# Gathering the first expert pair's tokens bank by bank, and requesting the third weight buffer in three parts

## The reference

```python
h = x + jnp.concatenate([a, c], axis=-1) @ w_out       # 1024 x 1024
return h + hier_moe(rms_norm(h, g_norm_ffn), ...)

def hier_moe(xn, w_router_group, w_router_expert, w_gate, w_up, w_down):
    t = xn.reshape(-1, D_MODEL)                        # 520 tokens
    lg = (t @ w_router_group)                          # 4 groups, top 1
    le = (t @ w_router_expert)                         # 8 experts in a group, top 2
    ...
    def expert_step(acc, ew):                          # 32 experts, 1024 -> 256 -> 1024
        wg, wu, wd, cw = ew
        h = jax.nn.silu(t @ wg) * (t @ wu)
        return acc + cw[:, None] * (h @ wd), None
```

## Time and profile before

| | |
|---|---|
| median of 3 runs | 611.67 us (610.62 to 613.29) |
| the profiled execution | 607.84 us, of which the span of instructions is 606.1 |
| PE busy | 553.9 us (91%) |
| DVE, ACT, POOL busy | 278.1, 166.8, 119.2 us |
| moved by DMA | 163.48 MB, mean 270 GB/s; HBM read 151.06 MB |

### The profile page before, as it was taken

One profiled execution on the slowest core, in us unless ns is written; L12 is line 12 of the kernel. 1 busy time (PEld: TensorE's weight loads), 2 busy tenths in 40 slices (PEclk: granted clock), 3 DMA queues, 4 the chain that ended last, 5 costly groups with the idle time before them and its releaser, 6 DMA issues.

```text
span 606.1 us, 8209 instructions
## 1 busy us (share of the span) xinstructions
PE 553.9 (91%) x2944; PEld 332.5 (55%) x2944; DVE 278.1 (46%) x681; ACT 166.8 (28%) x365; POOL 119.2 (20%) x124
## 2 busy tenths in 40 slices
PE   6999999998999999899999999999996869687992
PEld 4798899887675888744555853333332313232320
DVE  5887667968314787524358731111210111111256
ACT  7445344423312567610412210100100100000031
POOL 0488788310001000000000021111110111100013
PEclk9999999999999999899999999999997979898897
DMA  7990342599377900069600879999999999999874
GB/s 274 281 304 5 118 156 66 183 273 316 143 209 251 420 31 2 2 203 407 264 35 36 355 250 388 409 419 419 422 421 421 421 419 421 420 422 419 333 297 156
DMA packets 47159, 163.48 MB, mean 270 GB/s; under 512 B 8650, under 2 KB 22026, under 8 KB 35832
## 3 DMA queue, kind: packets, MB, share of 16 engines
q1 hardware_dynamic: 40448, 145.46, 63.2%
q0 software_dynamic: 6528, 17.01, 7.8%
q10 hardware_dynamic: 144, 0.52, 0.2%
HBM read 151.06 MB, written 19.76 MB: 282 GB/s over the span
## 4 chain that ended last, share of the span: by engine, by line
PE 47%; SPq 17%; DMA 11%; DVE 6%; POOL 3%; issue 3%; ACT 2%; POOLq 0%; DVEq 0%; ACTq 0%
SPq L512 11%; PE bank L1022 9%; PE bank L1085 9%; SPq L525 6%; DMA ring<-in_w_up_dram 5%; PE bank L1112 4%; PE bank L875 4%; DMA x<-q_rows 3%; PE bank L786 3%; PE bank L860 2%; DVE x L1445 2%; PE bank L808 2%; POOL ring L2139 2%; DMA hn_rows<-work 2%; PE bank L809 2%
## 5 line engine op out<-in xcount | busy, mean ns | idle before, releaser
L1085 PE MATMUL bank<-ring,work 128*64 128x512 f32 x512 | 122.8, 636 | 19.8 <-DMA ring<-in_w_up_dram 19.5
L1085 PEld LDWEIGHTS bank<-ring,work 128*64 128x64 f32 x512 | 39.6, 146 | 100.9 <-issue 87.1
L1445 DVE TENSOR_TENSOR work<-work,bank 128x256 f32<-128x256 f32 x16 | 6.7, 422 | 134.0 <-ACT work L1383 134.0
L1112 PE MATMUL bank<-ring,work 128*64 128x512 f32 x256 | 60.1, 612 | 7.6 <-ACT work L1387 7.6
L729 PE MATMUL bank<-split 128*128 128x384 f32 x192 | 66.1, 344 | 0.1
L730 PE MATMUL bank<-split 128*128 128x384 f32 x192 | 64.3, 335 | 0.0
L1022 PE MATMUL bank<-ring 128*128 128x512 f32 x96 | 42.6, 595 | 0.0
L1383 ACT ACTIVATE work<-bank 128x256 f32<-128x256 f32 x16 | 6.2, 385 | 128.2 <-PE bank L1085 128.2
L2139 POOL TENSOR_TENSOR ring<-ring 128x192 f32<-128x192 f32 (+1 forms) x40 | 38.8, 988 | 8.0 <-DVEq L1540 6.9
L1445 DVE TENSOR_TENSOR split<-ring,split 128x768 fp32r<-128x768 f32 (+1 forms) x35 | 37.3, 1099 | 6.4 <-PE bank L716 6.1
L1112 PEld LDWEIGHTS bank<-ring,work 128*64 128x64 f32 x256 | 17.3, 140 | 40.1 <-issue 28.7
(11 more groups left out here) (266 smaller groups left out, 832.9 us busy)
## 6 DMA issues: line engine op xcount, KB each, us to landing
ring<-in_w_down_dram SPq DMA_DIRECT2D x32, 1024.0 KB, 24.5
ring<-in_w_gate_dram SPq DMA_DIRECT2D x28, 1024.0 KB, 23.1
ring<-in_w_up_dram SPq DMA_DIRECT2D x28, 1024.0 KB, 25.2
ring<-in_w_in_dram SPq DMA_DIRECT2D x7, 1536.0 KB, 11.4
results<-work POOLq DMA_DIRECT2D x1, 4160.0 KB, 26.1
x<-in_x_prompt_dram SPq DMA_DIRECT2D x8, 512.0 KB, 13.1
ring<-in_w_out_dram SPq DMA_DIRECT2D x1, 4096.0 KB, 17.9
ring<-in_w_gate_dram SPq DMA_DIRECT2D x8, 512.0 KB, 13.2
```

The lines of the kernel that those rows point to most:

```text
L1085: last = pe.matmul(bank[2][64 * h:64 * h + 64, :], xgT[:, k, 64 * h:64 * h + 64], gate_up[s][h][:, :, k, :], start=(k == 0), stop=(k == KD ...
L1112: last = pe.matmul(bank[4 + j][64 * h:64 * h + 64, :], hT[:, c, 64 * h:64 * h + 64], down[s][h][:, c, j * 512:(j + 1) * 512], start=(c == ...
L1445: return dve.tensor_tensor(out, a, b, op)
```

## The change

Four places of the code differ.

First, on PE, the gathering products of pair 0. All products for bank 0 now come first. Then PE starts the gate and up products with their first four steps, and makes the products for bank 1 of tiles 1 to 4 and `tabulate` between step 3 and step 4 of `pair`. One of the clearing matmuls (line 970) also moves behind `count(3)`.

Second, on DVE, `tokens(0)` is split: the first half goes between `place(2)` and `place(3)`, and it no longer waits for the store of the last tile. That wait is moved to where ACT and DVE write the first result, and `hn` of the last tile lies 1024 elements further on in `work`, where the first result goes (it lay on `xgT`). `pick(2)` goes ahead of the last tile's `r_copy` and `choose(3)`.

Third, the layout of `w_out`: its column halves now lie one after the other, each 2 MB, and are requested by two transfers with rows of 2 KB.

Fourth, on SP, the third buffer is requested in three parts. The first half of the gates waits for the second group of the last tile in PE's order (`op_done` 18, after which the columns 0 to 511 of `w_out` are no longer read), then the downs for the third group, and the other gates for the fourth as before.

```diff
-        wout = cut(ring, 2 * SLOT, KD, D)
+        wout = [cut(ring, 2 * SLOT + j * 4096, KD, 512) for j in range(2)]
...
-        hn = [cut(work, at, D) for at in (0, D, 0, D, 3 * D)]
+        hn = [cut(work, at, D) for at in (0, D, 0, D, 4 * D)]
...
-            sp.dma_start(wout, w_out_v).then_inc(S["wout_in"], 16)
+            for j in range(2):
+                sp.dma_start(wout[j], w_out_v[:, :, j * 512:(j + 1) * 512]).then_inc(S["wout_in"], 16)
...
+            sp.wait_ge(S["op_done"], 4 * NT + 2)
+            gates((4, 5), 2, (0,))
             sp.wait_ge(S["op_done"], 4 * NT + 3)
-            gates((4, 5), 2, (0,))
             downs((4, 5), 2)
...
+            low_half, high_half = range(4), range(4, 8)
             pick_rows(0, range(0, 3))
             turn_h(4, (1,))
             count(2)
-            pick_rows(0, range(3, 5))
+            pick_rows(0, range(3, 4))
+            pick_rows(1, range(0, 1))
             route(4, (1,))
-            pick_rows(0, range(5, 8))
-            pick_rows(1, range(8))
-            pick_rows(2, range(4))
+            pick_rows(1, range(1, 4))
+            pick_rows(2, low_half)
+            pick_rows(3, low_half)
             count(3)
-            pick_rows(2, range(4, 8))
-            pick_rows(3, range(4))
-            pick_rows(4, range(4))
-            pick_rows(3, range(4, 8))
-            pick_rows(4, range(4, 8))
-            for b in range(len(GROUPS)):
-                tabulate(b)
+            pick_rows(0, range(4, 6))
+            pick_rows(4, low_half)
+            pick_rows(0, range(6, 8))
...
                 for k in range(KD):
+                    if first and k == KD // 2:
+                        for m in range(1, T5):
+                            pick_rows(m, high_half)
+                        for b in range(len(GROUPS)):
+                            tabulate(b)
                     if k == KD // 2:
                         pe.wait_ge(S["xg_evac"], 2 * i + 2)
...
-            def tokens(i, gain=gain_f):
+            def tokens(i, gain=gain_f, halves=(0, 1)):
-                if isinstance(i, int) and i == 0:
-                    dve.wait_ge(rows_moved[ORDER[NT]], 16)
-                else:
+                if not isinstance(i, int) or i > 0:
                     dve.wait_ge(S["gu_done"], i)
-                for g in range(2):
+                for g in halves:
...
             read_ranks(2)
+            pick(2)
             r_copy(4)
             choose(3)
-            pick(2)
             read_ranks(3)
             pick(3)
             place(2)
+            tokens(0, gains[:, 22:30], (0,))
             place(3)
...
-            tokens(0, gains[:, 22:30])
+            tokens(0, gains[:, 22:30], (1,))
...
             def result(i, s, turn):
                 if turn is not None:
                     dve.wait_ge(res_sem[s], turn)
+                elif i == 0:
+                    dve.wait_ge(rows_moved[ORDER[NT]], 16)
```

More of the change, by code:

```diff
@@ L909, in _ @@
                 last.then_inc(S["a_turned"], 1)
-            pe.wait_ge(S["wout_in"], 16)
+            pe.wait_ge(S["wout_in"], 32)
             pe.wait_ge(S["a_evac"], 2 * NT + 1)
@@ L1003, in _ @@
                     q = k // 2
-                    last = pe.matmul(bank[6 + j][32 * q:32 * q + 32, :], mixsT[:, k, :], wout[:, k, j * 512:(j + 1) * 512],
+                    last = pe.matmul(bank[6 + j][32 * q:32 * q + 32, :], mixsT[:, k, :], wout[j][:, k, :],
                                      start=(k % 2 == 0), stop=(k % 2 == 1))
@@ L1021, in out_group @@
                         src = attnT[:, k, t * P:(t + 1) * P] if k < NP else yT[:, k - NP, t * P:(t + 1) * P]
-                        last = pe.matmul(bank[g][:, :], src, wout[:, k, cols], start=(k == rng[0]), stop=(k == rng[-1]))
+                        last = pe.matmul(bank[g][:, :], src, wout[g % 2][:, k, :], start=(k == rng[0]), stop=(k == rng[-1]))
                 last.then_inc(S["op_done"], 1)
@@ L1392, in pair @@
                     act.wait_ge(res_sem[s], turn)
+                elif i == 0:
+                    act.wait_ge(rows_moved[ORDER[NT]], 16)
                 elif i == 1:
```

## The result

| | before | after |
|---|---|---|
| median, us | 611.29 (610.62 to 613.29, 6 runs) | 614.66 (613.22 to 617.76, 6 runs) |
| after / before | | 1.0076 [1.0050, 1.0102] |
| profiled execution, us | 607.84 (span 606.1) | 617.76 (span 616.0) |

The account below looks back on a forecast made before the run. The prediction took the expert-weight DMA stream (some 420 GB/s) as the bound, its early requests released by PE. Stream +1.1 us on the profiled 607.84 gives 608.9; 3.8 below the median, hence 612.7 us, range 608.3 to 616.2.

Parts of the forecast that it names:

- the likeliest case: The forecast itself: the weight stream moves by -1 to +2.5 us, ending at 610.7 to 614.5; chance 0.60.
- sign of being wrong: Second buffer's gates landing before 380 or after 385, or pair 14 or 15 changing its duration by over 2 us.
- X: Delay of pair 1's turn and the second buffer's gates request: 2.5 us; upper bound 7.2, lower bound a stream gain of 2.0.
- Third buffer and `w_out`: First gates requested at 327.8 instead of 333.72, worth nothing at the end by itself; `w_out` in two requests costs 0.
- First half of pair 0: Half of pair 0 done at 350.6 on PE, so SP's request goes at 350.65 instead of 355.59, 4.9 us earlier.
- Gather of pair 1: Table ready only after `tabulate`; gather takes 3.7 us, lands at 361.45, and PE waits 1.35 us.
- The room of 1.4: At the second buffer's gates request: stream 1.4 us behind what PE allows; a request X later moves it X - 1.4.
- Kept: Rival: SP's early first-half request carries its 4.9 us through whole, 606.8; chance 0.08.
- The gather comes late: Rival: pair 1's gather takes 6.4 us or more beside weights, end +3.8, 615.5, or 617.5 with slow clock; chance 0.14.
- the clock falls elsewhere: Rival: slow stretch misses the first down products, stream moves -0.6 to -3.6, 609.5 on the median; chance 0.18.
- the alternation: Late pairs alternate slow and fast, pair 14 slow by 3.0 us; turned round, up to 3.0 more comes off.

Follow-up runs that it names:

- e1: Kernel before, with only the new `w_out` layout in two requests and the third buffer requested in three parts: 609.44 us, 0.9979 of before.
- e11: Changed kernel with three unused products on PE ahead of pair 1's transposes, filling the wait for the gather: 615.43 us, 1.0084 of before.
- e6: Kernel before, with both halves of the first buffer's gates requested only after pair 0's last gate and up product: 610.65 us, 1.0005 of before.
- e8: Kernel before with the new `w_out` and third-buffer requests, the moved last-store wait, and `weigh` moved to pair 1: 608.66 us, 0.9974 of before.
- e10: Kernel before, with only the second buffer's gates request held until pair 1's down products are done: 613.82 us, 1.0063 of before.
- e4: Kernel before, with `weigh` (20 one-column product records) moved from pair 0 to pair 1 on PE: 609.91 us, 0.9983 of before.
- e2: Changed kernel with only its new PE and DVE order; `w_out` and the third buffer requested as before: 614.95 us, 1.0065 of before.
- e7: Changed kernel, with both halves of the first buffer's gates requested only after pair 0's gate and up products: 615.72 us, 1.0075 of before.
- e3: Changed kernel, with `tabulate` and the table ahead of bank 1's products and copy, so pair 1's gather is requested earlier: 614.81 us, 1.0060 of before.
- e5: Changed kernel, with the table ahead of bank 1's products and `weigh` moved to pair 1: 611.26 us, 1.0006 of before.

## Why the prediction was right and wrong

It forecast 612.7, slower by 1.1 us of stream, within the range 608.3 to 616.2; the median is 614.66. The sign was right and the path too: PE's early start is spent at once, and pair 1's gather delays the turn. The size was not: 5.5 us of delay instead of 2.5, and all of it went into the stream, 5.7 against the -1 to +2.5 of the likeliest case. The time lies just outside that case (610.7 to 614.5), and the kernel is slower by more than 0.5%, which had a chance of 0.16. The prediction's own sign of being wrong came true: the second buffer's gates land at A + 61.5, which is 385.9 counted from before's A (389.0 in its own profile) and past the 385 that it named. That the time still fell inside the range is owed to the wide bounds of X, not to the value that it took.

**Third buffer and `w_out`: right.** The first gates went at 330.86, which is A + 3.4 (predicted 327.8, A + 3.4). e1 shows no cost.

**First half of pair 0: 1.5 us too early.** I had h0 at 350.65, A + 26.2; it was A + 27.7. DVE waited 1.10 us for PE, which the prediction had not: the 16 gathering records ahead of `count(3)` took 3.27 us, where 16 of the same shape took 2.03 before, and the granted clock was 0.75 and 0.50 in the two windows from 344 to 348.

**Gather of pair 1: right.** The wait was 1.24 (predicted 1.35), the gather took 3.6 (3.7). The turn came at A + 38.6 instead of 37.0, mostly by the same 1.5.

**X: mis-sized, 5.5 against 2.5.** I took one slow stretch over unchanged, the first down products, and let it keep its 5.32. Of the missing 3.0, 1.6 is there at the turn already. Another 1.4 comes between the turn and the downs request (10.7 us against 9.3): 0.85 in the down products (6.17) and 0.5 in the transposes and `weigh`. e11 shows whose that is: with the wait for the gather filled it is gone. I had weighed that effect and left it out of the sum. By the Trainium skill (TensorE: Matmul & The Clock Gate, HAM oscillation) a wait for DMA between bursts makes the next burst start slow, and I said the sum would be nearer +3 by it. The 1.4 of e11 goes the way of that rule; but the eight transposes right behind the wait took 1.09 us, as before, and the slow products came after them; and the same wait ahead of pair 14 (3.4 to 3.5 us) was followed by products of 8.51 to 10.08 us in eight profiles and of 7.09 in three (e6, e8, e10). The bounds of X, up to 7.2, held both terms.

The other term, the 1.5 ahead of pair 0, has a pattern over all profiles, by two durations of records of the same shape:

| kernels | row of 16 gathering records ahead of the pair | first down products |
|---|---|---|
| before, e1, e6 | 2.03 | 5.28 to 5.35 |
| e4, e8, e10 | 3.40 to 3.56 | 3.65 |
| after, e2, e7, e11 | 2.94 to 3.58 | 5.35 to 6.17 |
| e3, e5 | 3.46, and 3.78 between the halves | 3.65 |

With the order of before the clock fell once in this stretch, early or late (six profiles). With the new order it fell twice (six of six). So the new order paid one more fall, 0.9 to 1.7 us in the 16 records alone, which no step of mine had. PE's work is the same in before, e1, e6 and e10, and e10 has the early fall and the others the late one, so the order of work alone doesn't fix its place. Why it falls where it does I cannot show. A wait of PE just ahead is not needed for it: in e7 the clock was 0.78 from 342 to 344 and 0.50 from 344 to 346, and PE was busy all through 338 to 346; and the late fall stood in before, e1 and e6, without a wait for a gather ahead of it. The section cited above speaks of waits alone; here the measurement goes further.

**The room of 1.4: right for one request, wrong as a rule.** This is the step that failed besides X. e10 gives 1.34. But in the kernels where all later requests came late, next to none of it reached the end: the gates were late by 5.5 (after), 6.5 (e2), 5.3 (e3), 3.4 (e5), 5.5 (e7) and 5.4 (e11), and pair 14 by 5.7, 6.4, 5.3, 3.2, 6.3 and 5.1. At the landing of the gates some room was there: in the kernel after they took 5.3 us instead of 6.2, so they landed 4.6 late, not 5.5. The prediction had taken 4.8. The other 1.1 was lost behind them. I had argued that the requests behind this one had slack. The bytes tell more. From A + 3 to A + 66:

```profile
327.41:390.41 63.00, 61.13 (x348) 34.46 (x349) 25.98 (x123) 10.77 (x20) 10.03 (x10) 0.97 0.84 322
```

```profile
330.49:393.49 63.00, 60.22 (x322) 34.83 (x323) 24.62 (x120) 9.99 (x18) 9.02 (x9) 0.92 0.80 290
```

The first is the kernel before, the second the one after. At 322 and 290 GB/s over 63 us that is 20.3 and 18.3 MB. The missing 2.0 MB are 4.7 us at 420 GB/s. The same sum gives 5.8 for e2 (pair 14: +6.4), 5.6 for e7 (+6.3), 4.6 for e3 (+5.3), 4.7 for e11 (+5.1), 4.0 for e10 (+3.9), 3.0 for e5 (+3.2) and 1.0 for e6 (+1.0). So the delay of the stream is the time that the queue stood empty ahead of it. In after that is two holes, 352 to 356 and 374 to 378, and a thin stretch at 356 to 366. Some 0.4 to 1.0 us more in after, e2, e3, e7 and e11 lie after A + 66; where is not settled.

**The rivals.** "Kept" is dead (e7). "The gather comes late" is dead as a mechanism (3.6 us), though the price it named, 615.5, was nearly met. Its dearer gather, 6.4 us, did come in e3 and cost nothing there, since PE was not yet done with the pair. Of "the clock falls elsewhere" the opposite half came true: it fell in a second place, not instead of the first. Pair 14 stayed slow (8.74), so the alternation was not turned round.

The 3.0 us that this rival hoped for there do not exist. In four kernels (e5, e6, e8, e10) pair 14 took the fast 7.09. The chain of waits then shows the scatter of its result landing that much later. Pair 14 in e6, then this scatter in before and in e6:

```profile
562.42 7.09 PE L1084 MATMUL bank<-ring,work 128*64 128x512 f32 x32 [3.47 <-DMA ring<-in_w_up_dram]
...
575.47 3.78 DMA results<-work,tbl
...
576.72 6.86 DMA results<-work,tbl
```

Pair 14 and the scatter together are 10.08 + 3.78 = 13.9 us in before and 7.09 + 6.86 = 14.0 in e6, and between 13.8 and 14.2 in all twelve profiles.

**What stays open** beside the clock: the stretch from A to the end is longer by 6.8 us in the profile of after and by 6.2 in e2, 5.9 in e11, while the timed ratios say 4.0 to 5.1. In after 5.7 of the 6.8 are pair 14's late start, and 1.1 are the reading back of the results at the end, 8.42 us against 7.33 (6.92 to 8.03 in the other kernels). Before and after:

```profile
580.46 7.33 DMA ring<-results
...
589.25 8.42 DMA ring<-results
```

Before has one profile, and its stretch may be a short one: e1, e4 and e8 come within 0.3 us of it and are timed 1.0 to 1.6 us faster. How much of the 5.7 us of stream shows in the time is thus known to a microsecond or two, no better.

## What to carry to other kernels

Where compute releases the requests of a stream, count bytes, not requests: an early request gains only if the queue does not empty behind it, and in e7 ten dry microseconds moved the stream by only 0.6 us more. Here, starting the first half of a step early delayed all that stood behind the second half, the table for the next gather and every request after it. Time the whole chain to the last request before the queue stays full, and let each stretch of small products have its slow duration as well as its fast one.

## What the runs showed of the hardware

The granted clock fell to 0.50 in a stretch where PE had been busy without a break (e7, 342 to 346), after transposes and products of 32 and 36 columns; 16 gathering records then took 2.94 to 3.58 us in the nine profiles with an early fall and 2.03 in the three without. A wait does not make the fall sure either: pair 14 took 7.09 us after a wait of 3.4 to 3.5 us in e6, e8 and e10, and 8.51 to 10.08 after the same wait in eight others. A wait of 1.24 us lengthened a slow stretch that was there without it by 1.4 us (10.7 us in after, e2 and e7 against 9.3 in e11). An indirect gather of 128 rows landed in 3.5 to 3.7 us into a queue that was empty or nearly so (seven profiles) and in 6.4 beside weights (e3). 1 MB of gates took 4.8 us into an empty queue, 5.0 to 5.3 in the kernels of the new order and 9.1 behind other weights (e4). `w_out` in rows of 2 KB instead of 4 KB costs nothing that the runs can tell (e1); its load is hidden by tens of microseconds, so this is no measure of the transfer itself.
